# A hybrid trunk kernel: every second transfer of eight first-half projections is multiplied in split form, its low half made by an accumulating transfer

## The reference

```
h = rms_norm(x, norm_g)
proj = h @ w_in                     # split into u_lru, u_s5, q/k/v of retention, q and kv of
                                    # sparse attention, gates, merge weights
y_lru, y_s5, y_ret, y_nsa = four token mixers over the projections
ys = stack(y_lru, y_s5, y_ret, y_nsa) * silu(gate_paths)
branch = einsum('bsnw,nwd->bsnd', ys, w_branch)
x = x + (sum_n sigmoid(merge_n) * branch_n) @ w_out
```

## Time and profile before

| | |
|---|---|
| median of 3 runs | 858.96 us (858.77 to 859.5) |
| the profiled execution's own time | 857.93 us |
| its span, first to last instruction | 856.1 us |
| TensorE busy | 825.7 us, 96% of the span |
| VectorE busy | 561.5 us, 66% |
| ScalarE busy | 312.2 us, 36% |
| GpSimd busy | 294.9 us, 34% |
| DMA, the SyncE queue | 125.88 MB, 48.4% of the 16 engines' span |
| mean granted TensorE clock | 0.987 |

### The profile page before, as it was taken

One profiled execution on the slowest core, in us unless ns is written; L12 is line 12 of the kernel. 1 busy time (PEld: TensorE's weight loads), 2 busy tenths in 40 slices (PEclk: granted clock), 3 DMA queues, 4 the chain that ended last, 5 costly groups with the idle time before them and its releaser, 6 DMA issues.

```text
span 856.1 us, 10220 instructions
## 1 busy us (share of the span) xinstructions
PE 825.7 (96%) x3918; PEld 611.4 (71%) x3918; DVE 561.5 (66%) x939; ACT 312.2 (36%) x519; POOL 294.9 (34%) x130
## 2 busy tenths in 40 slices
PE   8999999999899799999999999999998989999996
PEld 8864774446778688888888558644486867888885
DVE  2978999483697652634657889993828974435335
ACT  4411211015743545454425112110173534554542
POOL 1000000005567576767000000000157676665760
PEclk9999999999999899999999999999999998999999
DMA  8575544445245444444535745444554344445541
GB/s 250 140 245 144 192 127 122 130 141 201 94 127 168 123 148 148 120 152 152 153 70 161 244 119 198 143 125 127 146 172 147 116 132 129 137 130 170 172 147 50
DMA packets 86992, 126.56 MB, mean 148 GB/s; under 512 B 22072, under 2 KB 32672, under 8 KB 86944
## 3 DMA queue, kind: packets, MB, share of 16 engines
q1 hardware_dynamic: 86768, 125.88, 48.4%
q10 hardware_dynamic: 176, 0.04, 0.0%
HBM read 124.85 MB, written 1.05 MB: 147 GB/s over the span
## 4 chain that ended last, share of the span: by engine, by line
PE 59%; issue 29%; POOL 5%; DVE 3%; DMA 1%; ACT 1%; ACTq 0%; SPq 0%; POOLq 0%; DVEq 0%
PE proj L1480 29%; PE proj L1523 12%; PE proj L1519 6%; POOL w_lo L642 5%; PE M L1475 3%; PE M L1783 1%; PE M L1788 1%; DVE sc L1357 1%; PE M L1480 1%; DMA mt<-in_nsa_cv_w 1%; PE M L1753 1%; PE M L1807 1%; PE M L1806 1%; PE M L1624 1%; PE M L1805 1%
## 5 line engine op out<-in xcount | busy, mean ns | idle before, releaser
L642 POOL TENSOR_TENSOR w_lo<-raw,w_hi 128x1024 fp32r<-128x1024 f32 x112 | 286.3, 2586 | 504.9 <-ACT w_hi L660 473.9
L1523 PE MATMUL proj<-raw,h_full 128*128 128x512 f32 (+1 forms) x512 | 213.2, 572 | 0.0
L1523 PEld LDWEIGHTS proj<-raw,h_full 128*128 128x128 f32 x512 | 95.5, 190 | 104.7 <-issue 100.7
L660 ACT ACTIVATE w_hi<-raw 128x1024 fp32r<-128x1024 f32 x120 | 122.6, 1050 | 65.8 <-PE proj L1480 27.3
L1480 PE MATMUL proj<-w_hi,h_hi 128*128 128x512 f32 x320 | 128.4, 401 | 0.9 <-POOL w_lo L642 0.9
L1480 PE MATMUL proj<-w_lo,h_hi 128*128 128x512 f32 x320 | 124.9, 390 | 0.0
L1480 PE MATMUL proj<-w_hi,h_lo 128*128 128x512 f32 x320 | 124.8, 390 | 0.0
L1519 PE MATMUL proj<-h_full,raw 128*128 128x256 f32 x512 | 113.8, 381 | 0.0
L1519 PEld LDWEIGHTS proj<-h_full,raw 128*128 128x128 f32 x512 | 96.2, 190 | 14.1 <-issue 0.8
L1480 PEld LDWEIGHTS proj<-w_hi,h_hi 128*128 128x128 f32 x320 | 60.1, 188 | 14.4 <-issue 1.7
L1480 PEld LDWEIGHTS proj<-w_hi,h_lo 128*128 128x128 f32 x320 | 60.1, 188 | 13.0
(11 more groups left out here) (293 smaller groups left out, 1208.6 us busy)
## 6 DMA issues: line engine op xcount, KB each, us to landing
raw<-in_w_in SPq DMA_DIRECT2D x152, 512.0 KB, 3.5
raw<-in_w_branch SPq DMA_DIRECT2D x32, 512.0 KB, 3.8
raw<-in_w_out SPq DMA_DIRECT2D x16, 512.0 KB, 3.7
raw<-in_s_w_glu SPq DMA_DIRECT2D x8, 512.0 KB, 3.7
raw<-in_w_in SPq DMA_DIRECT2D x8, 256.0 KB, 2.6
merged<-in_nsa_ck_w SPq DMA_DIRECT2D x4, 512.0 KB, 5.3
mt<-in_nsa_ck_w SPq DMA_DIRECT2D x4, 512.0 KB, 6.9
merged<-in_nsa_cv_w SPq DMA_DIRECT2D x4, 512.0 KB, 5.8
```

The source lines that it names most:

```text
L642: nc.gpsimd.tensor_tensor(w_lo[:, slot(s, l), 0:n * w], raw[:, u % N_RAW, 0:n * w], w_hi[:, slot(s, l), 0:n * w].bitcast(f32), ALU.subtrac ...
L660: i = nc.scalar.activation(out_, in_, func, **kw)
L1523: last = mm(ps[:, 512 * t:512 * t + w], h_full[:, k, t * P:(t + 1) * P], rw, start=st_, stop=sp_, skip_group_check=True)
```

## The change

Of each of the eight chunks nsa_kv, gate_s5, gate_lru, merge_s5_0, merge_s5_1, ret_q, ret_k and nsa_q, the second and the fourth unit (those that start at row block 2 and 6) become split units: 16 units in a layer, called mixed units below. ScalarE casts such a unit to `w_hi` and then writes the negated `w_hi` to `w_lo`; GpSimd doesn't subtract but issues a transfer of the same weights from HBM, with addition, onto `w_lo`. The `raw` buffer of a mixed unit is free for the next load once the high half is cast. SyncE's loop is sorted anew: a mixed unit u is placed at u - 2.5. VectorE makes `h_lo` ahead of `scan_pair(1)`, and TensorE waits for it ahead of `nsa_kv`.

```diff
+HALF_NATIVE = ("nsa_kv", "gate_s5", "gate_lru", "merge_s5_0", "merge_s5_1", "ret_q", "ret_k", "nsa_q")
+def by_name(u):
+    return CHUNKS[UNITS[u][0]][0]
+MIXED_UNITS = [u for u in range(NU) if by_name(u) in HALF_NATIVE and UNITS[u][1] in (2, 6)]
+SPLIT_UNITS = [u for u in range(NU) if by_name(u) not in NATIVE or u in MIXED_UNITS]
+ADDED_UNITS = MIXED_UNITS
...
+def added_count(u, l):
+    here = slot(splits(u), l)
+    return sum((m, w) <= (l, u) and slot(splits(w), m) == here for m in range(DEPTH) for w in ADDED_UNITS)
...
             if u in VECTOR_UNITS:
                 eng.wait_ge(vlo_done, vector_splits(u + 1))
+            elif u in ADDED_UNITS:
+                eng.engine.wait_ge(lo_added[slot(splits(u), eng.l)], 16 * added_count(u, eng.l))
...
-                    for u in range(N_RAW, NU):
+                    for u in sorted(range(N_RAW, NU), key=lambda u: u - 2.5 if u in MIXED_UNITS else u):
...
-                        if u - N_RAW in SPLIT_UNITS:
+                        if u - N_RAW in ADDED_UNITS:
+                            sp.wait_ge(hi_done, splits(u - N_RAW + 1))
+                        elif u - N_RAW in SPLIT_UNITS:
                             wait_low(sp, u - N_RAW)
...
+                            if u in ADDED_UNITS:
+                                gp.wait_ge(neg_done, added_splits(u + 1))
+                                load_unit(pool, u, l, lo_added[slot(s, l)], w_lo[:, slot(s, l), 0:n * w], accum_op=ALU.add)
+                                continue
...
                             run(w_hi[:, slot(s, l), 0:n * w], raw[:, u % N_RAW, 0:n * w], ACT.Copy, hi_done)
+                            if u in ADDED_UNITS:
+                                act.wait_ge(hi_done, s + 1)
+                                run(w_lo[:, slot(s, l), 0:n * w], w_hi[:, slot(s, l), 0:n * w].bitcast(f32), ACT.Copy, neg_done, scale=-1.0)
...
                     i.then_inc(blk_ready, 1)
+                    for k in range(0, KD, 2):
+                        dve.wait_ge(hhi_done, k // 2 + 1)
+                        v.tensor_tensor(flat(h_lo[:, k:k + 2, :]), flat(h_full[:, k:k + 2, :]),
+                                        flat(h_hi[:, k:k + 2, :]).bitcast(f32), ALU.subtract).then_inc(hlo_done, 2)
...
-                            if name in NATIVE:
+                            if u not in SPLIT_UNITS:
                                 pe.wait_ge(raw_loaded[u % N_RAW], raw_target[u])
                             else:
                                 wait_low(pe, u)
...
+                    pe.wait_ge(hlo_done, KD)
                     chunk("nsa_kv", 0)
...
-                    pe.wait_ge(hlo_done, KD)
                     chunk("merge_s5_1", 0)
```

More of the change, by code:

```diff
@@ L69 @@
 NATIVE = ("u_s5", "cmp", "u_lru", "ret_v", "nsa_kv", "gate_s5", "gate_lru", "merge_s5_0", "merge_s5_1", "ret_q", "ret_k", "nsa_q")
-SPLIT_UNITS = [u for u in range(NU) if CHUNKS[UNITS[u][0]][0] not in NATIVE]
+HALF_NATIVE = ("nsa_kv", "gate_s5", "gate_lru", "merge_s5_0", "merge_s5_1", "ret_q", "ret_k", "nsa_q")
[3 more added lines that the diff above has]
+SPLIT_UNITS = [u for u in range(NU) if by_name(u) not in NATIVE or u in MIXED_UNITS]
 LO_ON_VECTOR = ("out_0b", "out_1b")
-VECTOR_UNITS = [u for u in SPLIT_UNITS if CHUNKS[UNITS[u][0]][0] in LO_ON_VECTOR]
+VECTOR_UNITS = [u for u in SPLIT_UNITS if by_name(u) in LO_ON_VECTOR]
+ADDED_UNITS = MIXED_UNITS
 def slot(s, l):
@@ L89, in vector_splits, with added_splits @@
     return sum(u < upto for u in VECTOR_UNITS)
+def added_splits(upto):
+    return sum(u < upto for u in ADDED_UNITS)
+def added_count(u, l):
+    here = slot(splits(u), l)
+    return sum((m, w) <= (l, u) and slot(splits(w), m) == here for m in range(DEPTH) for w in ADDED_UNITS)
 V_NORM, V_CONV, V_CONVB, V_BA, V_BX, V_LAM, V_D, V_BGLU, V_LR, V_LI, V_DT, V_ROWS = (
@@ L106 @@
     "lru_sqrt": 1, "mT_done": 2, "mag_arg": 1, "mag_exp": 1, "mhi_done": 2, "mlo_done": 2, "mt_free": 6,
[L107 to L113, removed]
+    "nT_done": 2, "nT_ready": 2, "neg_done": 16, "noT_done": 1, "no_cmp": 1, "nrope_ready": 2, "out_token": 2,
+    "qkT_done": 2, "qkT_ready": 2, "raw_loaded0": 448, "raw_loaded1": 448, "raw_loaded2": 448, "raw_loaded3": 448,
+    "rnT_done": 1, "rn_ready": 1, "ro_done": 4, "rope_ready": 2, "rrstd": 1, "rs_done": 4, "rs_ready": 4,
+    "rstd": 2, "rvar": 1, "s5_split": 2, "sq": 4, "th_ready": 1, "th_sin": 3, "trig_done": 24, "unit_used": 73,
+    "var": 2, "vbd_ready": 1, "vecT": 2, "vec_ready": 1, "vectors_loaded": 208, "vlo_done": 4, "wl_loaded": 64,
+    "xT_done": 4, "x_half": 3, "xc_ready": 1, "y_done": 8, "y_used": 4, "yg_hi": 4, "yg_lo": 4, "yg_ready": 4,
+    "yr_ready": 1, "z_arg": 1, "z_hi": 1, "z_lo": 1, "z_ready": 1, "z_tanh": 1}
 TWO_PI = 2.0 * math.pi
@@ L307, in hybrid_trunk @@
         chunk_done = sem("chunk_done")
+        neg_done = sem("neg_done")
+        lo_added = [sem(f"lo_added{i}") for i in range(N_SPLIT)]
         evacuated = [sem("evacuated0"), sem("evacuated1")]
@@ L381, in wait_low @@
                 eng.wait_ge(vlo_done, vector_splits(u + 1))
+            elif u in ADDED_UNITS:
+                eng.engine.wait_ge(lo_added[slot(splits(u), eng.l)], 16 * added_count(u, eng.l))
             else:
-                eng.wait_ge(lo_done, splits(u + 1) - vector_splits(u + 1))
+                eng.wait_ge(lo_done, splits(u + 1) - vector_splits(u + 1) - added_splits(u + 1))
         def pr(name):
@@ L409, in bc, with load_unit @@
             return ap.to_broadcast(shape)
-        def load_unit(sp, u, l, signal):
+        def load_unit(sp, u, l, signal, into=None, **how):
             c, k, n, w = UNITS[u]
             name = CHUNKS[c][0]
-            dst = raw[:, u % N_RAW, 0:n * w].rearrange("p (k n) -> p k n", k=n)
+            dst = (raw[:, u % N_RAW, 0:n * w] if into is None else into).rearrange("p (k n) -> p k n", k=n)
             def load(d, src):
-                sp.dma_start(d, src.rearrange("(k p) n -> p k n", p=P)).then_inc(signal, 16)
+                sp.dma_start(d, src.rearrange("(k p) n -> p k n", p=P), **how).then_inc(signal, 16)
             def w_in(col, width, d=None):
@@ L1166, in _ @@
                     scan_pair(5)
[L1167 to L1170, removed]
                     dve.wait_ge(evac("ck"), ev("ck"))
@@ L1524, in chunk @@
                                                       start=st_, stop=sp_, skip_group_check=True)
-                                elif kind == "u":
+                                elif name in ("u_s5", "u_lru", "gate_s5", "gate_lru"):
                                     for m in range(4):
```

2 lines of the change are left out of this document (1 added, 1 removed).

## The result

The changed kernel takes 866.63 us (median of 5 runs, 864.14 to 868.47), beside 858.77 of the kernel before on the same chip (857.87 to 859.5). The ratio is 1.0094, its 95% interval 1.0072 to 1.0116: slower by 0.9%. The profiled span went from 856.1 to 864.8 us.

The account below looks back on a forecast made before the run. TensorE, working in 96% of the span, was taken to bound the kernel. Terms summed to 0.0 us in the first layer and +0.8 in the second: 858.7 on the profiled execution, 859.8 as median; range 845 to 878.

Parts of the forecast that it names:

- The recorded signs of being wrong: Wait at unit 15 under 4 us, or accumulating transfers that land late or slow the plain ones.
- the mechanism at unit 15: Unit 17's load, placed ahead of ck and unit 15, delays unit 15: TensorE waits 7.3 us in each layer.
- the term for the transfer's bytes: Unit 17's accumulating transfer falls into the burst ahead of unit 15; its 0.52 MB take 1.35 us.
- the clock: After TensorE's wait at unit 15 the granted clock is low, costing 3.4 us a layer.
- My low end of 1.7: Low end of the clock cost behind unit 15, from an idle of 2.56 us: 1.7 us.
- the others 10 and more: Mixed units other than 19 and 29: accumulating landings may take 10 us and more before costing; taken at nothing.
- Rival 1: Accumulating is slow: landings over 6.1 us make TensorE wait at unit 19; 878 at 12 us, 888 at 14.4; chance 0.2.
- The wait at state_inputs(5): VectorE, busy 31.0 us without a gap, makes TensorE wait 2.4 us in the first layer, 2.0 in the second.
- cv: Its last transfer goes out sooner, so TensorE's waits of 1.4 and 0.2 us for it count as gone.
- h_lo: VectorE's split, 2.49 us, moved ahead of scan_pair(1), is covered by VectorE's wait of 3.45 us for TensorE.
- products: Native half's mixed units get shorter: 12 save 0.76 us each, 4 save 0.65; 11.7 us less a layer.
- rival 2: Loads keep up, unit 15 comes by 64.3: 839.2 us; half of it gives 848; chance 0.17 for both.

Follow-up runs that it names:

- The order alone: Kernel before, all units native, with only unit 17's load moved ahead of ck and unit 15: 874.89 us, ratio 1.0197.
- plain transfers: Changed kernel with the addition left out of GpSimd's transfers, same bytes, queue and moments: 857.27 us, ratio 0.9986.
- mending the order: Changed kernel with unit 17 loaded after unit 15, behind ck: 857.0 us, ratio 0.9985.
- the 841.93 us kernel: Changed kernel with unit 17 loaded after 15, unit 47 cast early, unit 19 native, cast of 23 behind nsa_kv's evacuation: 841.93 us, ratio 0.982.

## Why the prediction was right, and where not

**The number.** The forecast was 859.8 us; the kernel takes 866.63. That lies within 845 to 878, but just above the forecast's own 853.6 to 866, and it is slower by 0.9%, where 859.8 would have been hardly a change. The recorded signs of being wrong name accumulating transfers that land late, and they did: 8.5 us in the median, for the 4.9 that I took.

**Right: the mechanism at unit 15.** The load went out at 62.2 and landed 8.1 us later; TensorE waited 6.02 and 5.91, where I had 7.3, and 5.9 if the accumulating transfer does not disturb the burst. The order alone, without any such transfer, gives 5.71 and 5.89, so it hardly disturbed it. The size was off by 1.3 a layer, the term for the transfer's bytes.

**Mis-sized: the clock.** I took 3.4 us a layer, measured 1.95 and 1.6 (2.0 and 2.1 with the order alone, 2.6 and 2.3 with plain transfers, after the same wait). I scaled from a wait of 4.54 and its 7 us at the low clock, as if a longer wait left more behind. But here the low clock began at about 67.2, within the wait (64.4 to 70.4), and what of it falls into the wait costs nothing. My low end of 1.7, from the shorter wait, was the better.

**Failed: "the others 10 and more".** For unit 19 I worked the margin out as 6.1 us. The transfer took 8.29, and TensorE waited 2.14: the margin was right (6.2), the landing (4.9, for want of a row) was not. Unit 29 was given 8.7 and landed in 7.3: no wait. But I worked out margins for those two alone, and wrote the sentence on the others without doing it for unit 47. ScalarE, in order, does 47's cast at 192.5, behind the evacuation of the blocks; the transfer goes out at 195.15 and TensorE wants it at 201.2. Margin 6.0, landing 8.54, wait 2.56. Units 19 and 47 with the clock behind them cost about 8.4 us in the first layer; they are what moved +0.0 to +6.0. Casting 47 early removed its share, as predicted from this.

**Rival 1 came half true.** Landings passed 6.1 but not 12 (5.7 to 10.0 in the first layer). The two parts are of the same weight: mending the order takes 9.6 us off, taking the addition out of the transfer 9.4. My forecast named the first alone. It took the second at nothing, with 4.9 us from issue to landing in place of 8.5: that is the term which failed.

**VectorE: a near number by luck.** The wait at state_inputs(5) was 1.80 and 1.44 for 2.4 and 2.0, but it came another way. I had VectorE busy without a gap for 31.0 us. It took 34.3, from 84.61 to 118.95, with two idle times after its start:

```profile
84.61 0.69 DVE L1083 TENSOR_TENSOR sc<-M,sc 128x512 f32<-128x512 f32 x1 [9.57 <-PE M L1513]
95.91 0.48 DVE L1122 SCALAR_TENSOR_TENSOR qT<-u_s,vec,M 128x256 f32<-128x256 f32 x1 [1.14 <-PE M L1657]
98.32 0.62 DVE L1034 TENSOR_SCALAR sc<-const,small 128x256 f32<-128x256 f32 x2 [1.93 <-ACT sc L691]
```

Both stand behind the end of unit 19, the first through TensorE's next piece, the second through ScalarE's evacuation and cosines. Without these 3.1 us VectorE would have been done at 115.9, before TensorE came at 117.2. So the late unit 19 made TensorE wait twice. The sum that I had made is borne out in the 841.93 us kernel, where VectorE does not idle: 2.4 less 0.76 for a unit that stays native is 1.6, and TensorE waits 1.12 for cv and 0.50 at state_inputs(5).

**cv, h_lo, products.** cv's wait went in the first layer and stayed at 0.16 in the second. h_lo is free, shown by itself. The products gave 0.76 a unit; that a native unit beside split ones takes 0.1 longer was not in the sum, and its cause was not tested.

**The total** was within its range in part by luck, because the terms erred to both sides. In the first layer I had 1.3 and 1.5 too much at unit 15 and 0.6 at pair 5, and left out 8.4 and 1.0. And the split half gave back about 6 of the 14.8 us of both layers, for which the sum has no term. One slip: rival 2's 839.2 takes 20.6 us off the 859.8 of the forecast, in which +0.8 stands already; off the 858.96 of the kernel before it is 838.4.

## What to carry over

A load that is moved forward in a queue in order moves everything behind it to the moment at which its own buffer comes free: here one such load, in front of a burst for a unit with no slack, cost 16 us by itself, of the 23 that all the shorter units save. When a step gets a longer latency, work out the margin of every instance, and do it again after each repair, because the wait that is mended had given time to the next (unit 19: 2.1 us, then 6.3). A late unit can be paid for twice, once where it is waited for and once through the engine that evacuates it. And whether a unit frees its buffer by a cast or by its product decides when the unit four places on arrives: leaving one unit unsplit, which looked like a saving, cost 7.7 us until one cast was moved behind the evacuation that others wait for.

## What the runs showed of the hardware

- An accumulating transfer of 512 KB from DRAM lands in 8.5 us (median of 32; 5.7 to 10.0 in the first layer), the same transfer without the addition in 5.3, both issued by GpSimd; SyncE's take 4.1 in the same kernel. The addition takes 1.75 times the DMA engines' time, and keeps GpSimd for 1.22 us where the plain one takes 0.74.
- A GpSimd subtraction over 128x1024 stretched a VectorE step with both inputs in SBUF from 0.68 to 2.88 us, until 0.54 us after its own end, and did not stretch one that reads PSUM.
- In a wait of 6 us the granted clock fell to 0.50 before the wait was over; the unit after it took 5.48 instead of 3.53 us, hardly more than what a wait of 2.14 or 2.56 did to a split unit (4.62 and 4.57 instead of 2.77). In the second layer a wait of 1.44, with one of 0.16 before it, cost nearly as much (5.3 instead of 3.65); in the first a wait of 1.80 cost nothing (3.65).
